# Gate and output projections as three rounded products each, and a weight ring of three slots

## What is computed

```python
h = rms_norm(x, norm_mix)
proj = h @ w_in                        # 5936 columns for the mixers, then 4 x 1024 gate columns
...
y_nsa, y_sb, y_gla, y_fox = ...        # four attention-like mixers, 512 columns each
ys = jnp.stack([y_nsa, y_sb, y_gla, y_fox], axis=2)
branch = jnp.einsum('bsnc,ncd->bsnd', ys, w_branch)
gates = sigmoid(gate_logits + b_gate)                       # (1, 256, 4 * 1024)
mixed = jnp.sum(gates.reshape(B, S, 4, 1024) * branch, axis=2)
x = x + mixed @ w_out
h2 = rms_norm(x, norm_ff)
return x + jnp.square(jax.nn.relu(h2 @ w_ff1)) @ w_ff2
```

## Time and profile before

| | |
|---|---|
| runs | 2625.92, 2626.25, 2627.27 us; median 2626.25 |
| span of the profiled execution | 2632.6 us |
| PE busy | 2434.9 us, 92% |
| DVE busy | 1178.4 us, 45% |
| ACT busy | 1031.8 us, 39% |
| DMA | 341 MB, mean 130 GB/s |
| busiest PE lines | L261 461 us, L556 with w_in tiles 362 us |

### The profile page before, as it was taken

How to read it: one execution, slowest core, us unless ns; L and a number is a source line. 1 busy time by engine, 2 the same in 40 slices (tenths; PEclk the granted TensorE clock), 3 DMA queues, 4 the chain that set the end, 5 groups by cost and what they waited for, 6 DMA issues and landing times. The chain is left out here.

```text
span 2632.6 us, 31895 instructions
## 1 busy us (share of the span) xinstructions
PE 2434.9 (92%) x13191; PEld 1885.3 (72%) x13191; DVE 1178.4 (45%) x1672; ACT 1031.8 (39%) x1684; POOL 16.3 (1%) x23
## 2 busy tenths in 40 slices
PE   5999999989978999999989979889899999998998
PEld 4897667759868897667859855444688887454897
DVE  4465444235424464443335431456334335265456
ACT  3443224326424433225136424672422331344453
POOL 0000000000000000000000000000000000100000
PEclk9998999999998999999989979899999999999999
DMA  7433444644516425444535532101222223122352
GB/s 210 173 129 128 160 161 176 201 151 160 180 68 204 163 81 192 160 160 160 192 113 191 192 137 90 47 1 60 74 88 87 92 88 84 50 96 80 130 191 81
DMA packets 197137, 341.13 MB, mean 130 GB/s; under 512 B 45955, under 2 KB 60734, under 8 KB 196862
## 3 DMA queue, kind: packets, MB, share of 16 engines
q1 hardware_dynamic: 194300, 334.68, 36.2%
q0 software_dynamic: 944, 3.47, 0.4%
q10 hardware_dynamic: 1746, 0.89, 0.1%
HBM read 335.88 MB, written 3.15 MB: 129 GB/s over the span
## 5 line engine op out<-in xcount | busy, mean ns | idle before, releaser
L261 PE MATMUL bank<-hT_high,ring_low 128*128 128x256 f32 (+1 forms) x1520 | 461.2, 303 | 0.0
L556 PE MATMUL bank<-work,ring 128*128 128x256 f32 x1536 | 361.6, 393 | 8.4 <-DMA ring<-w_in 4.9
L556 PEld LDWEIGHTS bank<-work,ring 128*128 128x128 f32 x1536 | 295.5, 196 | 60.5 <-issue 20.5
L261 PEld LDWEIGHTS bank<-hT_high,ring_low 128*128 128x128 f32 x1520 | 291.8, 192 | 12.4 <-issue 0.5
L260 PE MATMUL bank<-ring_low,hidden_high 128*128 128x512 f32 x640 | 254.4, 397 | 0.0
L949 ACT ACTIVATE work<-bank 128x512 f32<-128x512 f32 (+6 forms) x260 | 121.9, 485 | 231.1 <-PE bank L262 175.7
L248 DVE TENSOR_TENSOR ring_low<-ring,half_high 128x2048 fp32r<-128x2048 f32 x64 | 146.4, 2292 | 136.8 <-ACT half_high L241 136.8
L556 PE MATMUL bank<-work 64*128 64x128 f32 (+8 forms) x1032 | 192.3, 336 | 4.6 <-DVE work L1266 4.4
L260 PE MATMUL bank<-hT_low,half_high 128*128 128x512 f32 (+1 forms) x512 | 176.9, 345 | 11.6 <-DVE hT_low L2300 8.2
L949 ACT ACTIVATE work<-bank,work 128x256 f32<-128x256 f32 (+1 forms) x200 | 88.2, 458 | 245.5 <-PE bank L556 155.7
L241 ACT ACTIVATE half_high<-ring 128x2048 fp32r<-128x2048 f32 x64 | 121.7, 1908 | 154.3 <-PE bank L262 154.3
(11 more groups left out here) (207 smaller groups left out, 4312.0 us busy)
## 6 DMA issues: line engine op xcount, KB each, us to landing
ring<-w_ff SPq DMA_DIRECT2D x32, 2048.0 KB, 8.1
ring<-mlp_w SPq DMA_DIRECT2D x32, 2048.0 KB, 8.2
ring<-w_in SPq DMA_DIRECT2D x30, 2048.0 KB, 9.4
ring<-w_ada SPq DMA_DIRECT2D x24, 2048.0 KB, 9.0
ring<-w_branch SPq DMA_DIRECT2D x6, 2048.0 KB, 14.3
ring<-w_in SPq DMA_DIRECT2D x32, 256.0 KB, 4.2
ring<-w_out SPq DMA_DIRECT2D x4, 2048.0 KB, 7.7
ring<-gqa_w_qkv SPq DMA_DIRECT2D x3, 2048.0 KB, 15.9
```

The lines of the kernel that those rows point to most:

```text
L261: nc.tensor.matmul(out, a[1], b[0], start=False, stop=False)
L556: return nc.tensor.matmul(out, lhsT, rhs, start=start, stop=stop)
```

## The change

- Gates: `gemm_T` with rounded products, 24 matmuls instead of 8. The parts of gate tiles join the list that `Split` cuts (numbers GATE_CUT = 26 and up, two per tile). The two parts of gate0 are cut at the end of the projection loops; in each step with odd i up to 27 ACT and DVE cut one further part.
- Output: w_out is cut too, in halves of four chunks of the contraction (numbers OUT_CUT and up), and so is `mixed` (`mixed_high` by ACT, `mixed_low` by DVE in `cut_mixed`). Each half h claims its two banks first, then works through both tiles of tokens for contraction half 0, then for half 1.
- The whole `hT` is no longer made. The return of x to the chip waits for the last gate, g31.
- Ring: gate tiles alternate between slots 0 and 1, ada tiles use slot 2, branches and out tiles slots 0, 2, 1, 0, 2, 1. Slot 3 stays the place of the high buffers until up3, the fourth feed-forward tile, which waits for the end of the output. The order of the loads is now by the step that needs them.

```diff
-    step_fills, step_tiles = [], []
+    step_fills = []
...
+    needed = [(4 * i - 3, "gate", i) for i in range(KD)] + [(i, "ada", n) for n, i in enumerate(ada_steps)]
+    step_tiles = [(kind, n) for _, kind, n in sorted(needed)]
...
-    first_whole = [tile[0] for tile in tiles].index("gate0")
-    slots = [n % (N_SLOTS - 1) for n in range(first_whole)] + [(N_SLOTS - 1 + n) % N_SLOTS for n in range(len(tiles) - first_whole)]
-    W = Weights(sem, "w", chip["ring"], slots, tiles, {"gate0": done("ff")})
+    first_step = [tile[0] for tile in tiles].index("gate0")
+    slots = [n % 3 for n in range(first_step)]
+    slots += [n % 2 if kind == "gate" else 2 for kind, n in step_tiles]
+    slots += [0, 2, 1, 0, 2, 1]
+    feed = [0, 2, 1, 3]
+    slots += [feed[n % N_SLOTS] for n in range(len(tiles) - len(slots))]
+    W = Weights(sem, "w", chip["ring"], slots, tiles, {"up3": done("wo11")})
...
+    GATE_CUT = sum(len(ranges) for _, ranges, _ in cuts)
+    cuts += [(f"gate{i}", wide, [f"g{4 * i + 1}", f"g{4 * i + 3}"]) for i in range(KD)]
+    OUT_CUT = GATE_CUT + 2 * KD
+    cuts += [(f"out{h}", [("k", 0, 4), ("k", 4, 4)], [5 + h, f"wo{h}1"]) for h in range(2)]
...
-            back_at = W.order["branch2"]
+            back_at = W.order["branch3"]
...
-            sp.wait_ge(hT_whole, 1)
+            sp.wait_ge(*done("g31"))
...
-                    w = W.arrived(pe, f"gate{i // 4}")
+                    w = Y.arrived(pe, f"gate{i // 4}", i % 4 // 2 * 256)
                     ps = PROJ.claim(pe, f"g{i}")
-                    if i == 0:
-                        pe.wait_ge(hT_whole, 1)
-                    for k in range(KD):
-                        last = mm(ps[:, 0:S], w[:, k, i % 4 * P:(i % 4 + 1) * P], hT[:, k, :], k == 0, k == KD - 1)
-                    last.then_inc(PROJ.full, 1)
+                    gemm_T(ps[:, 0:S], w, slice(i % 2 * P, i % 2 * P + P)).then_inc(PROJ.full, 1)
...
-            pe.wait_ge(mixed_ready, 3 * KD // 2)
             for h in range(2):
-                w = W.arrived(pe, f"out{h}")
-                for t in range(TT):
-                    ps = PROJ.claim(pe, f"wo{h}{t}")
-                    for k in range(KD):
-                        last = mm(ps[:, :], mixedT[:, k, t * P:(t + 1) * P], w[:, k, :], k == 0, k == KD - 1)
-                    last.then_inc(PROJ.full, 1)
+                banks = [PROJ.claim(pe, f"wo{h}{t}") for t in range(TT)]
+                for b in range(2):
+                    w = Y.arrived(pe, f"out{h}", 4 * b)
+                    for t in range(TT):
+                        for k in range(4):
+                            if h == 0 and t == 0 and k % 2 == 0:
+                                pe.wait_ge(mixed_cut, 2 * b + k // 2 + 1)
+                            c = 4 * b + k
+                            last = product(nc, banks[t][:, :], [part[:, c, t * P:t * P + P] for part in (mixed_high, mixed_low)],
+                                           [part[:, k, :] for part in w], c == 0, c == KD - 1)
+                        if b == 1:
+                            last.then_inc(PROJ.full, 1)
+                    if b == 0:
+                        last.then_inc(half_used, 1)
...
+                    if i % 2 == 1 and i < 4 * KD - 4:
+                        Y.make_high(nc, act, GATE_CUT + 2 + i // 2)
...
+            Y.make_high(nc, act, OUT_CUT, OUT_CUT + 1)
+            for fc in range(KD // 2):
+                part = slice(2 * fc, 2 * fc + 2)
+                act.wait_ge(mixed_whole, fc + 1)
+                copy(mixed_high[:, part, :], mixedT[:, part, :]).then_inc(mixed_rounded, 1)
+            Y.make_high(nc, act, OUT_CUT + 2, OUT_CUT + 3)
             X.make_high(nc, act, 0, 1)
...
-            Y.make_low(nc, dve, 25)
+            Y.make_low(nc, dve, 25, GATE_CUT, GATE_CUT + 1)
 
             for t in range(TT):
                 silu_gate(t)
...
-            vec.tensor_tensor(hT, hT_low[:, :, :].bitcast(F32), hT_high[0][:, :, :].bitcast(F32), ALU.add).then_inc(hT_whole, 1)
...
+                if i % 2 == 1:
+                    Y.make_low(nc, dve, GATE_CUT + 2 + i // 2)
...
-                    vec.tensor_tensor(mixed, mixed, part, ALU.add).then_inc(mixed_ready, 1)
-                if n > 0:
+                    vec.tensor_tensor(mixed, mixed, part, ALU.add).then_inc(mixed_ready if n < 3 else mixed_whole, 1)
+                    if n == 3 and fc >= 1:
+                        cut_mixed(fc - 1)
+                    if n == 3 and fc == 1:
+                        Y.make_low(nc, dve, OUT_CUT + 1)
+                if 0 < n < 3:
                     dve.wait_ge(mixed_ready, 4 * n)
+                if n == 2:
+                    Y.make_low(nc, dve, OUT_CUT)
+            cut_mixed(KD // 2 - 1)
+            Y.make_low(nc, dve, OUT_CUT + 2, OUT_CUT + 3)
             X.make_low(nc, dve, 0, 1)
             dve.wait_ge(x_back, 16)
```

More of the change, by code:

```diff
@@ L361, in first_layer @@
     hT_high = [chip["hT_high"], rounded("hT_high2", after_hT, KD, S)]
+    mixed_high, mixed_low = rounded("mixed_high", after_hT - KD * S, KD, S), rounded("mixed_low", qk_at, KD, S)
     x_kept = out.rearrange("b (t p) d -> p (b t) d", p=P)
@@ L381, in first_layer @@
     ada_steps = [i for i in range(4 * KD) if i % 8 in (1, 4, 6)]
-    step_fills, step_tiles = [], []
+    step_fills = []
     for i in range(4 * KD):
-        if i % 4 == 0:
-            step_tiles.append(("gate", i // 4))
         step_fills.append(f"g{i}")
@@ L392, in first_layer @@
             step_fills.append(f"ada{ada_steps.index(i)}")
-            step_tiles.append(("ada", ada_steps.index(i)))
+    needed = [(4 * i - 3, "gate", i) for i in range(KD)] + [(i, "ada", n) for n, i in enumerate(ada_steps)]
+    step_tiles = [(kind, n) for _, kind, n in sorted(needed)]
     LV = [f"lv{n}_{par}" for n in range(len(LEVELS)) for par in range(2)]
@@ L519, in first_layer @@
     x_saved, x_back = sem("x_saved"), sem("x_back")
-    hT_whole = sem("hT_whole")
+    mixed_whole, mixed_rounded, mixed_cut = sem("mixed_whole"), sem("mixed_rounded"), sem("mixed_cut")
     hT_cut = sem("hT_cut")
@@ L1356, in _, with cut_mixed @@
                     .then_inc(prob_ready, 1)
+                if i % 2 == 1:
+                    Y.make_low(nc, dve, GATE_CUT + 2 + i // 2)
+            def cut_mixed(fc):
+                part = slice(2 * fc, 2 * fc + 2)
+                dve.wait_ge(mixed_rounded, fc + 1)
+                vec.tensor_tensor(mixed_low[:, part, :], mixedT[:, part, :], mixed_high[:, part, :].bitcast(F32), ALU.subtract)\
+                    .then_inc(mixed_cut, 1)
             for n in range(4):
```

## The result

The changed kernel took 2637.72 us (median of 4 runs, 2636.8 to 2641.54), the kernel before 2626.76 beside it. The ratio is 1.0040 with a 95% interval of 1.0026 to 1.0054: slower by 0.4%, 11 us. The prediction was 2633.5 in 2616 to 2650, slower with 0.55.

A forecast was written before the change was run, and what follows sets the result against it. PE was taken to bound the gate stage, with ACT and DVE chains deciding at two turns. Terms -34.0 + 26.5 + 0 + 0.4 + 12.4 + 2 = +7.3 us gave a 2633.5 us median, range 2616 to 2650.

The forecast's parts named there:

- A: Gate products in the steps: 24 rounded matmuls at 0.118 us make a gate cost 3.03 us; -34.0 us in all.
- D: Cuts of gate weights by ACT and DVE in the steps: nearly all hidden under PE; +0.4 us.
- F: PE clock in the steps: shorter gates bring one more low-clock stretch in all; +2 us.
- B: Start of attention: silu gates and fox bias queue behind gate0's cut, 13.25 us later per layer; +26.5 us.
- C: Ring of three slots for weight loads in the steps: all loads stay hidden; 0 us.
- E: Output: second half waits 10.1 us for residual adds behind DVE's cuts, then runs at low clock; +12.4 us.
- Rival 3: Gates and output: rounded products run at array time, 0.109 us and down to 0.131; 2600 to 2620 us, chance 0.03.
- Rival 2: Start of attention: ACT cuts the first gate tile at once, without waiting for "ff"; 2619.5 us, chance 0.10.
- Rival 5: Steps: ring of three starves PE, three waits of 4 us per layer for late gate tiles; 2657 us, chance 0.04.
- Rival 1: Output: no wait between halves, as DVE's residual adds run before its cuts; 2610 us, chance 0.07.
- rival 4: PE clock: more low-clock stretches, in most fox steps and after every gap; 2638 to 2655 us, chance 0.14.

## Why the prediction was right, point by point

Differences of medians give each part its size, since every kernel differs from the next by one part (the first two by the gates and the ring together): before 2626.9, rounded gates with a late cut 2597.1, gate0 cut early 2624.8, rounded output as changed 2637.2.

| term | predicted | by medians | by ratios |
|---|---|---|---|
| A, D and F, gates in the steps (measured with C in it) | -31.6 | -29.8 | -32 |
| B, start of the attention | +26.5 | +27.7 | +27 |
| C, ring of three, alone | 0 | +2.7 | +2, within -2 to +6 |
| E, output | +12.4 | +12.4 | +15 |
| sum of A to F, C counted once | +7.3 | +10.3 (whole kernels: +11.0, +11.6) | +11 |

Each measured size is uncertain by some 4 to 7 us. The signs and the order of the terms are shown; where the missing 3 or 4 us lie is not, since the two columns put them in different terms. That each term came out within 3 us is better than these measurements can tell, and in part luck.

- **A** held in its step: 3.02 us where an ada product follows, for 3.03. The row of the projections was the right price. The Trainium skill, "TensorE: Matmul & The Clock Gate", Back-to-back issue gap, leads to 109 ns for a single matmul of 256 columns, without the load of its weights. The trace does not agree: 117 ns between the last products. For a stream with weight loads at 512 columns the same section of the Trainium skill has 131 ns per matmul. The trace does not agree here either: 48 products in 11.3 us, 235 ns each, in the second half of the kernel with the adds first. Rival 3 falls with both. Gate 1 alone was mis-sized: it took 4.3 and 4.8 us in the two layers, in the second profile 5.4 and 4.9, for 5.1.
- **B** held to the row: cut behind ACT's copy, 12.7 later at the fox bias and 13.5 at gate 1 for 13.25. The 0.8 between the two is not B's: the kernel with gate0 cut late has it too, and so has the ring alone. Bounds 9.1 and 15; the split of 9 and 4 was shown by moving the silu gates alone. Rival 2 (a copy at once) falls, since ACT's copy started at 228.28.
- **C** held for the loads: no wait of PE for a tile, in the changed kernel or with the ring alone, and a load lands sooner than before. Rival 5 falls. Its 0 left something out, though. The prediction says that the end of gate 0's wait for its tile gives nothing. By the rows it costs 0.8 us per layer, since PE is then idle at another place and the transposes behind it run at the low clock. One layer in the second profile of the kernel before also has these transposes at 1.89 us, and there too it is 19.8 from the fox bias to gate 1. Of the 2.6 us that the ring alone costs by its rows, these 1.6 stand in the changed kernel too. Beside the clock (F) they are the only part of the missing 3 or 4 that rows point to, and no time clear of the noise shows them.
- **D** held: PE's waits in the steps are the same as before. Its +0.4 us was put down without a sum, and no run is fine enough to show it.
- **E** held in its mechanism, and in the gap to a tenth of a microsecond (10.03 for 10.1). The second half took 14.1 and 12.8 us in the two layers, 13.0 and 13.2 in the second profile, for the forecast 13.1. By the rows that makes 12.8 and 12.1 us for the two layers together, for 12.4. That the medians also say 12.4 is luck; the ratios say 15. Rival 1 was the kernel that I then built; it measured 2611 where the rival had 2610.
- **F** is open. Gates of 3.5, 3.5 and 4.9 us stand at 389, 413 and 431 in the first layer, and of 4.7, 4.3, 4.4 and 4.2 at 1052, 1166, 1190 and 1207 in the second; the forecast was of gates over 5 us in the fox steps, and there is none. The kernel before has long gates as well (5.4 us in the first layer and 5.7, 5.6 and 4.1 in the second; in its second profile 5.6, 5.5 and 4.0 in the first and none found in the second). The mean clock from 262 to 490 us is 0.96 for the kernel before's 0.99. Windows of the kernel before, then of the changed one:

```profile
262.00:490.00 228.00, 227.88 (x1191) 158.98 (x1190) 94.94 (x191) 88.68 (x218) 0.00 (x0) 0.99 0.45 160
1035.00:1260.00 225.00, 225.00 (x1153) 156.51 (x1152) 90.10 (x183) 85.67 (x209) 0.00 (x0) 0.96 0.45 159
```
```profile
262.00:490.00 228.00, 225.77 (x1514) 168.31 (x1513) 131.99 (x219) 119.07 (x247) 0.00 (x0) 0.96 0.54 184
1035.00:1260.00 225.00, 224.68 (x1494) 168.54 (x1495) 130.28 (x219) 114.66 (x243) 0.00 (x0) 0.95 0.52 176
```

If all work there were bound by the clock, 0.03 of 228 us would be 6.8 us in the first layer and 0.01 of 225 would be 2.3 in the second, more than the term's 2. But the second profile of the kernel before has 0.96 and 1.00 in the same two windows, and that of the changed kernel 0.96 and 0.97, so the profiles of one kernel differ by as much as the two kernels do. No run changed the clock alone. How many microseconds it holds, and whether rival 4 came in part (it began at 2638, and the medians are 2637.7 and 2636.7), is not shown.

One step besides was wrong, without harm: carrying the profile's 6.35 us to the median. It compared a span with times of runs (the run of that span took 2634.40, 8 above the median), and took one run's distance from the median for a fixed one. The changed kernel's profiled run does not lie above its median, so the span forecast at 2639.9 came out 5 lower (2635.0) while the median came out 4 higher.

## What to carry to other kernels

When work is added to an engine that has room on average, ask what stands behind it in that engine's order. Two 2 us cuts cost 13 us per layer because short work that had been hidden was queued behind a cut that waited for another engine; the same cuts a few lines later cost nothing that the runs show. And before a result is claimed in pairs of banks, put the reads that free the pair ahead of anything that can wait: a gap of 10 us, 9 more than needed, cost 11.9 and 10.6 in the two layers, since TensorE came out of it at half its clock. Last, a wait that goes away off the critical path is not always free: it can leave the engine idle, and at a low clock, at a place that is on it.

## What the runs showed that was not expected

- The profiled execution of the kernel before lay 8 us above its median twice (runs 2634.40 and 2635.37, median 2626.84), that of the changed kernel 1 to 3 below its own. With runs of one kernel up to 17 us apart that can be chance.
- With the new slots and the new order a gate tile landed in 7.6 us for 12.9, with no gain in time.
- The trace calls "issue" what looks like a bank claim. With the adds first, the last add that frees a bank begins at 558.89 and takes 0.69, and PE starts at 559.68, 0.1 after its end; the row of PE names no engine. Here the add:

```profile
558.89 0.69 DVE L1420 TENSOR_TENSOR x_sb<-x_sb,bank 128x512 f32<-128x512 f32 x1 [0.66 <-PE bank L262]
```
